# Query projection from raw fp32 weights, a reordered start of the expert gathers, a new opening and a new last expert step

## The reference, cut to what matters

```python
h = layernorm(x, ln_in_g, ln_in_b)
proj = h @ w_in                       # 2048 x 7184, mixer (conv and mLSTM heads)
h = layernorm(ALPHA * h + mix @ w_out, ln1_g, ln1_b)
# expert layer: 8 heads, per token
q = (h @ wq).reshape(-1, 8, 2, 128)
s = einsum('thpc,hpnc->thpn', q, keys)
sv, si = top_k(s, 16)                 # per half, then 16 of the 256 sums
ue, ve = u[eid], v[eid]               # rows of 2048 floats
act = gelu(einsum('thkd,td->thk', ue, h))
ff = einsum('thk,thkd->td', gate * act, ve)
h = layernorm(ALPHA * h + ff, ln2_g, ln2_b)
# second block: rmsnorm, h @ w_in_2, two more mixers, w_out_2, gated FFN, rmsnorm
```

## Time and profile before

| what | us |
|---|---|
| median of 3 runs | 3084.77 (3082.28 to 3091.47) |
| the profiled execution's own time | 3083.94 |
| its span, first to last instruction | 3082.2 |
| PE busy / DVE busy / ACT busy | 2675.2 / 1758.7 / 886.4 |
| bytes moved | 859.96 MB, mean 279 GB/s |

### The profile page before, as it was taken

One profiled execution on the slowest core, in us unless ns is written; L12 is line 12 of the kernel. 1 busy time (PEld: TensorE's weight loads), 2 busy tenths in 40 slices (PEclk: granted clock), 3 DMA queues, 4 the chain that ended last, 5 costly groups with the idle time before them and its releaser, 6 DMA issues.

```text
span 3082.2 us, 33252 instructions
## 1 busy us (share of the span) xinstructions
PE 2675.2 (87%) x12565; PEld 1917.4 (62%) x12565; DVE 1758.7 (57%) x2230; ACT 886.4 (29%) x964; POOL 545.4 (18%) x532
## 2 busy tenths in 40 slices
PE   6999998787777777777777689999999999999998
PEld 6999878732222222222222237998877888888886
DVE  5456557855555555555555545544656556565445
ACT  3433443311000011111111013543444444444443
POOL 0000001443433343333334530000000000000000
PEclk9999999999999999999999899999999999999999
DMA  6554556999999999999999984544454555555553
GB/s 229 168 174 156 186 178 243 365 422 421 421 422 421 422 422 422 421 422 422 422 422 422 422 355 148 167 162 151 137 192 163 191 189 189 187 187 187 193 195 144
DMA packets 222090, 859.96 MB, mean 279 GB/s; under 512 B 17616, under 2 KB 24112, under 8 KB 149168
## 3 DMA queue, kind: packets, MB, share of 16 engines
q0 software_dynamic: 73728, 536.90, 42.0%
q1 hardware_dynamic: 148272, 321.79, 31.2%
HBM read 856.54 MB, written 2.10 MB: 279 GB/s over the span
## 4 chain that ended last, share of the span: by engine, by line
PE 59%; DMA 29%; DVE 6%; issue 3%; ACT 2%; POOL 1%; POOLq 0%; DVEq 0%; ACTq 0%
DMA vb<-in_peer_v,vidx 27%; PE PS L506 11%; PE PS L2122 8%; PE PS L2284 8%; PE PS L508 5%; PE PS L535 5%; PE PS L539 5%; PE PS L537 5%; PE PS L553 4%; PE PS L557 4%; PE PS L555 4%; DMA ub<-in_peer_u,uidx 2%; DVE wl L421 2%; ACT wh L416 1%; DVE ub L1525 1%
## 5 line engine op out<-in xcount | busy, mean ns | idle before, releaser
L2122 PE MATMUL PS<-vb,diag 128*128 128x512 f32 x1920 | 896.4, 611 | 316.1 <-DMA vb<-in_peer_v,vidx 304.6
L421 DVE TENSOR_TENSOR wl<-raw,wh 128x2048 fp32r<-128x2048 f32 x290 | 664.6, 2292 | 719.0 <-ACT wh L416 718.6
L2122 PEld LDWEIGHTS PS<-vb,diag 128*128 128x128 f32 x1920 | 350.7, 192 | 861.7 <-issue 739.0
L1525 DVE CUSTOM_DVE_ANT_0 ub<-ub,RES 128x2048 f32<-128x2048 f32 x256 | 586.3, 2292 | 476.5 <-DMA ub<-in_peer_u,uidx 472.8
L416 ACT CAST wh<-raw 128x2048 fp32r<-128x2048 f32 x290 | 552.8, 1907 | 858.4 <-PE PS L539 268.1
L506 PE MATMUL PS<-XHL,wh 128*128 128x512 f32 x1408 | 488.2, 394 | 0.1
L753 POOL DMA_INDIRECT ub<-in_peer_u,uidx x256 | 274.6, 1073 | 663.2 <-DVE uidx L1513 497.9
L535 PE MATMUL PS<-XHL,wh 128*128 128x256 f32 x1344 | 384.1, 286 | 7.0 <-DVE XHL L595 4.6
L508 PE MATMUL PS<-XHL,wl 128*128 128x256 f32 x1408 | 390.0, 277 | 0.0
L539 PE MATMUL PS<-XHL,wl 128*128 128x256 f32 x1344 | 381.4, 284 | 0.0
L537 PE MATMUL PS<-XHL,wh 128*128 128x256 f32 x1344 | 381.3, 284 | 0.0
(11 more groups left out here) (345 smaller groups left out, 2277.3 us busy)
## 6 DMA issues: line engine op xcount, KB each, us to landing
raw<-in_w_in SPq DMA_DIRECT2D x112, 1024.0 KB, 5.1
raw<-in_w_ffn_gate SPq DMA_DIRECT2D x44, 1024.0 KB, 5.2
raw<-in_w_ffn_up SPq DMA_DIRECT2D x44, 1024.0 KB, 5.2
raw<-in_w_ffn_down SPq DMA_DIRECT2D x44, 1024.0 KB, 4.8
raw<-in_w_out SPq DMA_DIRECT2D x32, 1024.0 KB, 5.1
raw<-in_peer_wq SPq DMA_DIRECT2D x16, 1024.0 KB, 6.0
ub<-in_peer_u,uidx POOLq DMA_INDIRECT x256
vb<-in_peer_v,vidx POOLq DMA_INDIRECT x244, 15.3
```

Source lines behind the costliest of these rows:

```text
L421: dve.tensor_tensor(wl[u % 2][:], raw[u][:], wh[u % 2][:].bitcast(F32), ALU.subtract).then_inc(lo_full[u % 2], 1)
L1525: dve.tensor_tensor_reduce(ub[k % RING][:], ub[k % RING][:], RES[:, tb, :], 1.0, 0.0, ALU.mult, ALU.add, dots[:, tb, k:k + 1]).then_inc(S. ...
L2122: m = pe.matmul(PS[:, 4 * tb + b, :], diag[:, k, :], vb[k % RING][:, b * W:(b + 1) * W], start=False, stop=False, skip_group_check=True)
```

## The change

1. Query projection: no `wh`/`wl` and no divided activation. ACT copies the turned `h` to `XF` in fp32 (`h_out`), and PE multiplies raw fp32 weights in one fp32 matmul per chunk and tile. The four units of `S_OUT + 3`'s divided halves are held in `ubr` and not in `raw`, so the first loads of `peer_wq` need not wait for PE. All twelve splits of the later three slabs, and four of the first, go from ACT and DVE. `S_WQ` is gone from the slab count.
2. First expert steps: 12 u rows of step 1, not 4, precede the v rows of step 0; then one u row follows every fourth v row. DVE runs whole `expert_step`s during the projection.
3. Opening: gain and bias come as 32 rows of 128 (`GB`), PE turns them to columns (`gbc`); token block 0 is normalised by ACT (`centre_x`), block 1 by DVE (`tensor_scalar`); ACT applies gain and bias after the turn (`first_hi`). The spread gain and bias are loaded after the first weights and applied to the residual in slab 3 (`residual_gain`, `residual_bias`).
4. Last step: v rows use `ub` and `raw` (eight buffers); rows 0-3, 8, 10, 12-15 go to DVE, six to PE. `last_row` k 0 to 3 are issued a little earlier. Units 2 and 3 of `S_IN2` are loaded only when rows 12 and 13 are used.

```diff
-DVE_ROWS = (0, 1, 2, 5, 7, 9, 11, 13)
+DVE_ROWS = (0, 1, 2, 3, 8, 10, 12, 13, 14, 15)
...
     def last_slot(k):
+        if k % (2 * RING) < RING:
+            return k % RING
+        return RING + (k if k < 2 * RING else k + 2) % RING
...
         load_x(0)
+        sp.dma_start(GB[0:DC, :], inp["ln_in_g"].rearrange("(c p) -> c p", p=P)).then_inc(S.gb_in, 16)
+        sp.dma_start(GB[DC:2 * DC, :], inp["ln_in_b"].rearrange("(c p) -> c p", p=P)).then_inc(S.gb_in, 16)
         load_x(1)
-        sp.dma_start(GAIN[:], row(inp["ln_in_g"], D)).then_inc(S.gain_in, 16)
-        sp.dma_start(BIAS[:], row(inp["ln_in_b"], D)).then_inc(S.norm_in, 16)
...
+        def centre_x():
+            act.wait_ge(S.shift_ready, 1)
+            for q in range(4):
+                y = slice(q * W, q * W + W)
+                act.activation(RES[:, 0, y], RES[:, 0, y], ACT.Identity, bias=nshift[:],
+                               scale=rstd[:, 0:1]).then_inc(S.xhat, 1)
+        def first_hi(u):
...
+            for c in range(UC):
+                d = u * UC + c
+                act.activation(XA[:, u % 2, c, :], x_wide(d), ACT.Identity, bias=gbc[:, DC + d:DC + d + 1],
+                               scale=gbc[:, d:d + 1]).then_inc(S.xa_ready, 1)
+            act.wait_ge(S.xa_ready, UC * u + UC)
+            act.copy(XH[:, u * UC:u * UC + UC, :], XA[:, u % 2, :, :]).then_inc(S.xt_hi, 2)
...
         def q0_unit(tb, u):
             for c in range(2 * UC):
                 d = u * 2 * UC + c
-                pe.matmul(o, XH[:, d, y], hi[:, c, :], start=d == 0, stop=False)
-                pe.matmul(o, XH[:, d, y], lo[:, c, :], start=False, stop=False)
-                m = pe.matmul(o, XL[:, d, y], hi[:, c, :], start=False, stop=d == DC - 1)
+                m = pe.matmul(PS[:, 4 + 2 * tb, 0:2 * P], XF[:, d, y], narrow(raw[u])[:, c, :], start=d == 0,
+                              stop=d == DC - 1)
...
+        def query_slab(j):
+            if j >= 2:
+                pe.wait_ge(q_copied, j - 1)
+            for u in range(UNITS):
+                pe.wait_ge(raw_whole[u], 16 * (j + 1))
+                for t in range(4):
+                    for c in range(UC):
+                        d = u * UC + c
+                        m = pe.matmul(cm_out(j % 2)[:, t, :], raw[u][:, c, t * P:t * P + P], XF[:, d, :],
+                                      start=d == 0 and t % 2 == 0, stop=d == DC - 1, skip_group_check=True)
+                m.then_inc(q_used, 1)
+                if u == 0:
+                    scores(2 * j)
+                    scores(2 * j + 1)
...
             if first and k == 0:
-                pool.wait_ge(w_free[1], 2 * S_WQ + 8)
+                pool.wait_ge(q_used, UNITS * 4)
...
-        for k in range(RING):
+        for k in range(3 * RING):
             u_row(1, 1, k, False)
         for k in range(TOPK):
             v_row(0, 0, k, True)
-            if k + RING < TOPK:
-                u_row(1, 1, k + RING, False)
+            if k % RING == RING - 1:
+                u_row(1, 1, 3 * RING + k // RING, False)
...
+        dve.wait_ge(S.scores_cp, 2)
+        expert_step(0, 0, 0)
+        dve.wait_ge(S.scores_cp, 3)
+        expert_step(1, 1, 1)
```

More of the change, by code:

```diff
@@ L805, in _ @@
             v_row(LAST - 1, 0, k, False)
-        for k in range(RING):
-            v_row(LAST - 1, 0, TOPK // 2 + 2 * k, False)
-            v_row(LAST - 1, 0, TOPK // 2 + 2 * k + 1, False)
-            last_row(k)
+        for k, before in ((8, ()), (9, (0,)), (10, (1,)), (11, (2,)), (12, ()), (13, (3,)), (14, ()), (15, ())):
+            v_row(LAST - 1, 0, k, False)
+            for j in before:
+                last_row(j)
         for k in range(RING, TOPK):
@@ L956, in _ @@
         scores_out(0)
-        x_hi(act, 1, 4, 8)
-        split_hi(act, S_WQ, 2)
+        h_out(1)
         soft(0, 0)
         q0_out(1)
-        split_hi(act, S_WQ, 3)
         q0t_out(1)
         scores_out(1)
-        split_hi(act, S_WQ + 1, 0)
         pq_head()
-        split_hi(act, S_WQ + 1, 1)
-        run_slabs(act, split_hi, S_WQ + 1, 3, plan(
-            each(pq_out, S_WQ + 1, 3),
-            [(q, 0, lambda n=n: scores_out(n)) for q in range(3) for n in (2 * q + 2, 2 * q + 3)],
-            [(2, 0, lambda: soft(1, 1))]))
-        act.activation(adiag[:], ident[:], ACT.Copy, scale=ALPHA).then_inc(S.base_diag, 1)
+        scores_out(2)
+        scores_out(3)
+        soft(1, 1)
+        pq_out(1)
+        scores_out(4)
+        scores_out(5)
+        act.wait_ge(S.dots_ready, 1)
+        act.activation(acts[:, 0, :], dots[:, 0, :], ACT.Gelu).then_inc(S.gelu_ready, 1)
+        pq_out(2)
+        scores_out(6)
+        scores_out(7)
+        pq_out(3)
         scores_out(8)
         scores_out(9)
+        act.activation(adiag[:], ident[:], ACT.Copy, scale=ALPHA).then_inc(S.base_diag, 1)
         def weigh(n, tb, first=False, rows=range(TOPK)):
-            act.wait_ge(S.dots_ready, n + 1)
-            act.activation(acts[:, tb, :], dots[:, tb, :], ACT.Gelu).then_inc(S.gelu_ready, 1)
+            if not first:
+                act.wait_ge(S.dots_ready, n + 1)
+                act.activation(acts[:, tb, :], dots[:, tb, :], ACT.Gelu).then_inc(S.gelu_ready, 1)
             act.wait_ge(S.ew_ready, n + 1)
@@ L1437, in _ @@
         first_norm(0)
-        split_lo(dve, S_WQ, 0)
-        x_lo(dve, 1, 0, 4)
-        split_lo(dve, S_WQ, 1)
         first_norm(1)
@@ L1563, in _ @@
         keys_first()
-        x_lo(dve, 1, 4, 8)
         keys_next()
@@ L1661, in _ @@
         dve.wait_ge(S.ew_ready, LAST + 1)
-        for k in DVE_ROWS[:3]:
+        for k in range(4):
             last_row(k)
@@ L1668, in _ @@
         second_norms(0)
-        for k in DVE_ROWS[3:-1]:
-            last_row(k)
-        x_lo(dve, 2, 0, 4)
-        last_row(DVE_ROWS[-1])
+        last_row(8)
+        x_lo(dve, 1, 0, 4)
+        last_row(10)
+        last_row(12)
         for q in range(4):
@@ L2058, in q1_tile @@
                 d = (u % 2) * 2 * UC + c
-                pe.matmul(o, hi[:, c, x], XH[:, d, :], start=d == 0 and t == 0, stop=False, skip_group_check=True)
-                pe.matmul(o, hi[:, c, x], XL[:, d, :], start=False, stop=False, skip_group_check=True)
-                m = pe.matmul(o, lo[:, c, x], XH[:, d, :], start=False, stop=d == DC - 1, skip_group_check=True)
-            return m
+                m = pe.matmul(cm_out(0)[:, t, :], narrow(raw[u])[:, c, t * P:t * P + P], XF[:, d, :],
+                              start=d == 0 and t == 0, stop=d == DC - 1, skip_group_check=True)
```

324 lines of the change are left out of this document (182 added, 142 removed).

## The result

The changed kernel takes 3066.75 us (median of 7 runs, 3058.81 to 3071.31) against 3084.77 us (7 runs, 3082.27 to 3094.74): ratio 0.9929, 95% interval 0.991 to 0.9947. The sign of the prediction was right. By the medians the gain is 18.0 us, half of the 36.8 that it said; between like runs (next paragraph) it is 24.3, two thirds. 3066.75 lies above the 3065 of its stated range, though inside the 3067 that its own bounds add up to.

The account below looks back on a forecast made before the run. The prediction took PE to bound the projections and DMA gathers the expert steps. From the profiled 3083.9 us it took 10.4 (opening), 20.9 (rows) and 5.7 (last step), giving 3046.9, plus 0.8 for the median: 3048 us, range 3037 to 3065.

Parts of the forecast that it names:

- Opening: Start of the kernel: PE's first projection matmul at 18.4 us instead of 28.87; -10.4 us, bounds -7 and -12.
- Plain fp32: Query projection: an fp32 pair of 256 columns takes 0.44 us, a unit 7.04 us against 5.7 for fp32r.
- Rival (b): Query projection: fp32 weight loads not hidden, v rows 51 us later; +14 us, 3099 us; chance 0.05 with its half-exposed case.
- To the first gather: Queries to first u row: indices 5.7 us earlier, from 0.9 us on PE and DVE work taken away.
- Projection and u rows: Query projection beside gathers: weight loads take 31 us of DMA time, 28 u rows fit, PE's last use of XF at 596.6.
- 8.4 rows: Gathers issued by 650.5: 9.2 rows more, less 0.8 for the stream's new start; -20.9 us, including 5.7 of earlier indices.
- The forecast's test for a miss: Signs of being wrong: PE gaps behind ACT in the projection, DMA share under 0.9 there, or `second_norms(0)` waiting for `GAIN3`.
- Rival (a): Projection: four-buffer u ring too slow, 4.5 us a row, stage gains only -10; 3059 us; chance 0.16 with the ACT-wait rival.
- (a) to (d): Rival (a), Rival (b), query-stage change gives nothing (3069 us, chance 0.05), ACT wait for dots stops PE 10 to 20 us.
- v rows bound by PE: After the projection: PE sets the pace at 3.44 us a v row, sixteen rows from 608 to 663 us.
- Last step: Last expert step: last gather lands about 1838.5, not 1845.2, then DVE bounds; -5.7 us, bounds -1 and -8.

Follow-up runs that it names:

- run 5: Only the new opening put into the kernel before, all else as it was; median 3074.50 us, ratio 0.9971 to the kernel before.
- run 1: Changed kernel with the later three query weight slabs alternating between eight buffers, not four; median 3045.34 us, ratio 0.9872 to the kernel before.
- run 2: Changed kernel without the twelve weight loads of query slabs 1 to 3 and PE's waits for them; median 3046.73 us, ratio 0.9876.
- run 10: Changed kernel with query slabs 2 and 3 paired so weight loads come in 4 KB pieces, same four buffers; median 3051.26 us, ratio 0.9862.
- run 7: On run 1, all 16 u rows of step 1 precede the v rows of step 0, not 12; median 3049.91 us, ratio 0.9895.
- run 3: Changed kernel with four u rows of step 1 ahead of the v rows, not twelve; median 3077.52 us, ratio 0.9959.
- run 6: On run 1, DVE's `x_lo` in the last step moved behind rows 10 and 12; median 3048.18 us, ratio 0.9888.
- run 8: On run 6, last-step row 14 goes from DVE to PE and DVE takes row 13 before the sums; median 3045.42 us, ratio 0.9881.
- run 9: Changed kernel with eight weight buffers, 16 u rows ahead, two early v rows, late `x_lo`, row 14 on PE; median 3055.40 us, ratio 0.9891.

## Why the prediction was right in sign and its gain too large

It said 3048 us and 3066.75 were measured. 12.7 of the 18.8 us belong to the change (37.0 forecast, 24.3 between like runs), the rest to the FFN's rate.

- **Opening**: -10.4 forecast, -9.9 at PE's start, -10.2 at the end when made alone (run 5). Right.
- **Plain fp32**: 0.44 us a pair; measured 6.91/16 = 0.43. Rival (b) is dead. The Trainium skill's rule on weight loads ("TensorE: Matmul & The Clock Gate", "Packing small matmuls") would have made it 0.66, by the estimate of the prediction from that page's load time; the trace disagrees.
- **To the first gather**: -5.7 and the opening, 16.1; measured 15.95. Right.
- **Projection and u rows: the step that failed.** It gave weight loads "their share" of the DMA engines as bytes over 422 GB/s, left u rows 3.84 us each (its own 28.6 rows in 102 us would be 3.6), and never asked when a load lands. Measured: u rows 3.28 us each, loads 24.9 us from issue to landing where four buffers allow some 21; 7.2 us of waits behind loads and 5.1 of low clock; slabs in 101.4 us, not 89; v row 15 at 650.00, not 639.6. Runs 1, 2 and 10 take the cause away in three ways and find 10.9 to 11.7 us at v row 15.
- **Rows and stamps.** Of these 10.4 us the sum misses only 8.0 at the end of `second_norms(0)` (23.3 us gained, 31.3 forecast). From v row 15 to that point both kernels take the same time, 1153.1 and 1153.3 us, so the forecast's own stamp, 33.9 us earlier, was worth 33.9; counted as 8.4 rows it was put at 31.3. That this term was 2.6 us too small made the miss smaller, by luck.
- **The forecast's test for a miss** looked for a DMA share under 0.9 in the projection, and while PE waited the share was 1.01 to 1.04: engines full of gathers, with PE waiting for the same engines. It fell to 0.16 only from 590 on, when the u rows had run out. Rival (a) even had weight loads as what helps the ring. None of (a) to (d) was this case; that the shorter runs took the 3059 us of (a) is chance, since the u rows were fast and not slow.
- **v rows bound by PE**: 3.44 us forecast, 3.46 measured (128 records from 607.53 to 662.9), and runs 2 and 7 confirm that PE alone sets this stretch. Right, as is that the order is worth something: four u rows ahead cost 9 to 11 us more (run 3).
- **Last step**: -5.7 forecast, -5.0 measured. `GAIN3` was not waited for. That DVE bounds it was half right: in run 6 the landing of the last rows did so as much.
- **Clock behind it**: 2.2 us lost from the aggregate to the third `split_lo`, and 1.7 near 2160, in no term of the sum. What brings these falls of the clock stays open: runs 8 and 9 have neither, run 1 only the second. With them 8.0 + 0.7 + 3.9 = 12.6 of the 12.7 us are placed.
- The rest of the distance to 3066.75 is the FFN's rate in four of seven runs, in no term of the sum.

Runs 1, 8 and 10 beat both kernels: 3045.34, 3045.42 and 3051.26 us, lowest 3045.06, 3042.52 and 3046.88. Run 10 needs no buffer more.

## What to carry to other kernels

Before a split or a wait is taken away that held gathers back, ask which plain loads shared the DMA engines with them: a ring of gathers that never runs dry takes most of the engines' time, and loads in small pieces land several times later than they did beside a slower stream (24.9 us for 5.6). Compare a load's time to landing under that load with (buffers - 1) x the time of a unit; past it, take more buffers or longer contiguous pieces; either removed the waits here. A DMA share of 1 says that the engines are busy, not that they carry what the bound engine waits for.

## What the runs showed of the hardware

- A 1 MB load in pieces of 2 KB took 5.6 us to land beside gathers that came at 177 GB/s, and 24.9 us beside gathers that filled their queue (306 GB/s). With pieces of 1 KB it took 32.0 us, with pieces partly of 4 KB 19.6.
- Two waits of 3.1 and 3.0 us on PE were followed by stretches at the lower clock (0.83, 0.80 and 0.86 over 540 to 570), which cost another 5.1 us. After 19.2 us of idleness the same work took 27.4 to 28.0 us in five runs and 29.9 to 30.4 in three whose clock fell once more.
- The FFN's 1408 pairs of fp32r matmuls ran at one of two rates, 488.2 or 497.6 us, at a granted clock of 1.00, 488.2 in nine of the thirteen profiled executions and 497.6 in four. No kernel was profiled at both, but the times of most fall into two groups about 10 us apart. What chooses between them stays open.
